# Router and token gather moved ahead of the last norm, and the experts' down weights kept in two pairs of tiles

## The reference, cut to what matters

```python
mod = silu(c) @ w_ada + b_ada                  # 6 * 1024 numbers
sh_m, sc_m, g_m, sh_f, sc_f, g_f = split(mod)
...                                            # mixer of the last block
x = x + g_m * (mixed @ w_out)
h = rms(x, norm_ffn) * (1.0 + sc_f) + sh_f     # rms: x * rsqrt(mean(x*x) + 1e-6) * norm_ffn
logits = h @ w_router + b_router               # 256 x 32
top_val, top_idx = top_k(logits, 4)
gates = softmax(top_val)
for e in range(32):                            # tokens of expert e only
    gu = h[tokens_e] @ w_gu[e] + b_gu[e]       # 1024 -> 2048
    g, u = clipped halves of gu
    act = (u + 1.0) * (g * sigmoid(1.702 * g))
    out = act @ w_dn[e] + b_dn[e]              # 1024 -> 1024
x = x + g_f * (sum over experts of gate * out)
```

## Time and profile before

| | |
|---|---|
| median of 3 runs | 1702.54 us |
| profiled execution | 1703.73 us, its span 1701.9 us |
| TensorE busy | 1580.8 us, 93% |
| VectorE, ScalarE busy | 394.1 us, 298.8 us |
| granted TensorE clock, mean | 0.98 |
| HBM read | 511.2 MB |
| expert loads | 192 pieces of 2 MB |

### The profile page before, as it was taken

One profiled execution on the slowest core, in us unless ns is written; L12 is line 12 of the kernel. 1 busy time (PEld: TensorE's weight loads), 2 busy tenths in 40 slices (PEclk: granted clock), 3 DMA queues, 4 the chain that ended last, 5 costly groups with the idle time before them and its releaser, 6 DMA issues.

```text
span 1701.9 us, 19443 instructions
## 1 busy us (share of the span) xinstructions
PE 1580.8 (93%) x7907; PEld 921.5 (54%) x7907; DVE 394.1 (23%) x889; ACT 298.8 (18%) x584; POOL 19.5 (1%) x40
## 2 busy tenths in 40 slices
PE   7989999998999999979999999989999998999995
PEld 6858787785887778853343434333333333343332
DVE  2442113412444381122111111111111111111101
ACT  1324104223222431021011101110100101011010
POOL 4000000000000000000000000000000000000000
PEclk9999999998999999979999999999999999999998
DMA  9764644546322424359999999999999999999994
GB/s 266 177 219 162 225 171 159 191 145 236 131 100 75 149 99 148 128 178 403 427 427 428 429 428 429 428 429 428 429 428 429 429 427 429 428 429 428 429 428 177
DMA packets 83752, 515.04 MB, mean 303 GB/s; under 512 B 4872, under 2 KB 8248, under 8 KB 59128
## 3 DMA queue, kind: packets, MB, share of 16 engines
q1 hardware_dynamic: 82488, 513.43, 74.9%
q0 software_dynamic: 1184, 0.92, 0.7%
q10 hardware_dynamic: 32, 0.01, 0.0%
HBM read 511.20 MB, written 3.15 MB: 302 GB/s over the span
## 4 chain that ended last, share of the span: by engine, by line
PE 73%; DMA 19%; DVE 4%; ACT 3%; issue 1%; SPq 0%; DVEq 0%; ACTq 0%
PE psum L450 25%; PE psum L1033 20%; DMA ring<-in_w_gu 16%; PE psum L1102 9%; PE psum L1006 4%; PE psum L459 3%; DMA ring<-in_w_in 2%; PE psum L1016 2%; PE psum L1024 1%; PE psum L509 1%; PE psum L490 1%; PE psum L595 1%; ACT hiddenT L1515 1%; ACT hg L1504 0%; PE psum L484 0%
## 5 line engine op out<-in xcount | busy, mean ns | idle before, releaser
L1033 PE MATMUL psum<-ring,hg 128*64 128x512 f32 x2048 | 458.7, 596 | 21.5 <-DMA ring<-in_w_gu 21.5
L450 PE MATMUL psum<-hT,ring 128*128 128x256 f32 x1504 | 337.1, 384 | 4.7 <-ACT hT L1298 4.3
L450 PEld LDWEIGHTS psum<-hT,ring 128*128 128x128 f32 x1504 | 287.5, 193 | 52.9 <-issue 13.0
L1033 PEld LDWEIGHTS psum<-ring,hg 128*64 128x64 f32 x2048 | 139.0, 137 | 312.7 <-issue 267.6
L1102 PE MATMUL psum<-w_down,hiddenT 128*64 128x512 f32 x1024 | 229.2, 600 | 28.2 <-ACT hiddenT L1515 25.2
L1102 PEld LDWEIGHTS psum<-w_down,hiddenT 128*64 128x64 f32 x1024 | 74.9, 138 | 162.1 <-issue 162.1
L1959 DVE TENSOR_SCALAR gu<-psum 128x512 f32<-128x512 f32 x32 | 22.1, 692 | 529.3 <-PE psum L1033 529.3
L1511 ACT ACTIVATE hidden<-gu 128x512 f32<-128x512 f32 x32 | 20.2, 630 | 316.4 <-DVE gu L1959 316.4
L1006 PE MATMUL psum<-pick,h_tok 128*128 128x128 f32 x512 | 63.3, 284 | 2.9 <-DVE passes L1942 2.9
L459 PE MATMUL psum<-ring,hT 128*128 128x260 f32 (+2 forms) x192 | 60.4, 470 | 6.0 <-DMA ring<-in_w_in 6.0
L1006 PEld LDWEIGHTS psum<-pick,h_tok 128*128 128x128 f32 x512 | 60.3, 197 | 8.1 <-issue 5.0
(11 more groups left out here) (381 smaller groups left out, 1170.9 us busy)
## 6 DMA issues: line engine op xcount, KB each, us to landing
ring<-in_w_gu SPq DMA_DIRECT2D x128, 2048.0 KB, 22.6
w_down<-in_w_dn SPq DMA_DIRECT2D x64, 2048.0 KB, 20.8
ring<-in_w_in SPq DMA_DIRECT2D x24, 2048.0 KB, 8.8
ring<-in_w_ada SPq DMA_DIRECT2D x12, 2048.0 KB, 9.3
ring<-in_w_out SPq DMA_DIRECT2D x6, 2048.0 KB, 7.9
ring<-in_w_in SPq DMA_DIRECT2D x2, 2064.0 KB, 16.4
ring<-in_w_ssm_o SPq DMA_DIRECT2D x2, 2048.0 KB, 8.4
ring<-in_w_in SPq DMA_DIRECT2D x1, 2112.0 KB, 12.2
```

Source lines behind the costliest of these rows:

```text
L450: mm = pe.matmul(bank[0:m, c * T:(c + 1) * T], w[:, k, c0 + c * P:c0 + c * P + m], src[:, k, :], start=(i == 0), stop=(i == k_n - 1))
L1033: mm = pe.matmul(psum[half * CAP:(half + 1) * CAP, 4 + part, :], hg[:, k, side, :], w[:, c0:c0 + 512], start=False, stop=(k == KC - 1), sk ...
```

## The change

The norm of the second half of the last block is no longer applied before router and gather. Since the norm is a factor for each token (1/rms) and a factor and a shift for each feature, it is taken apart:

- The router multiplies `xT` itself by `w_scaled`, which is `w_router` times the factor of each feature. The shift's part of the logits is added to `b_router` beforehand. The factor 1/rms of each token (`row_rstd`) multiplies the logits on VectorE.
- The eight chunks' products go to four groups of 32 columns of the array (partitions 0 to 31, 32 to 63, ...), the squares likewise; four small matmuls (`token`) add the four groups up and turn them into rows of tokens.
- `h_tok` holds the rows of `xT`. `pick` holds 1/rms in place of 1, and ScalarE applies factor and shift of each feature when it reads the gathered tokens, in eight activations instead of two.
- Factor and shift by feature in the order of the gather come from `ffn_rows`, 16 matmuls on columns of `mod_rows` taken 8 apart, and 8 for the shift's logits, behind `dt` in the last block. `b_ada` is loaded by GpSimd as 12 rows and added to `mod_rows` before it is turned; `norm_ffn` is loaded twice, once as `(c p) -> p c`, once as `(p k) -> p k`.
- The four best experts are marked with a match instead of a threshold, a running sum and a comparison.
- The matmuls with `b_dn` stand ahead of the first gather, which uses banks 6 and 7.
- The down weights have four tiles, a pair for each side (one of the four is the space of `hT` and `wide`). Both pairs are loaded before the first expert; in the loop the down pieces of an expert are loaded ahead of its gate and up pieces.

The core of the diff:

```diff
+        def ffn_rows():
+            bank = take("rows")
+            for k in range(KC):
+                lhs = mod_rows[:, k:512:KC]
+                for half in range(2):
+                    mm = pe.matmul(bank[half * HEAD:half * HEAD + HEAD, 12 * k:12 * k + 12], lhs,
+                                   K["mod_sum"][:, :], start=True, stop=True)
+            full(mm, "rows")
+            bank = take("base")
+            for k in range(KC):
+                mm = pe.matmul(bank[:, 0:NE], modT[:, 24 + k:25 + k].broadcast_to([P, P]), w_router[:, k, :],
+                               start=(k == 0), stop=(k == KC - 1))
...
-        norm_sums("f.", None)
-        pe.wait_ge(ev("h_ready"), 4 * (DEPTH + 2))
-        bank = take("router")
...
+        for c in range(KC):
+            if c % 2 == 0:
+                read_out(pe, f"wo{c // 2}")
+            q = slice(32 * (c % 4), 32 * (c % 4) + 32)
+            mm = pe.matmul(psum[q, banks["router"][0], 0:T], w_scaled[:, c, :], xT[:, c, :],
+                           start=(c < 4), stop=(c >= 4), skip_group_check=True)
...
+            if c % 2:
+                pe.wait_ge(ev("sq_d"), 4 * norm_sums.n + c // 2 + 1)
+                for c1 in (c - 1, c):
+                    q = slice(32 * (c1 % 4), 32 * (c1 % 4) + 32)
+                    mm = pe.matmul(psum[q, banks["squares"][0], 0:T], ones[:, 0:32], wide[:, c1, :],
+                                   start=(c1 < 4), stop=(c1 >= 4), skip_group_check=True)
...
         # ScalarE, gathered tokens
-                act.activation(hg[:, 4 * part:4 * part + 4, 0:width, :], bank[:, :, 0:width, :], ACT.Copy)
+                for k in range(4 * part, 4 * part + 4):
+                    ins = act.activation(hg[:, k, 0:width, :], bank[:, k % 4, 0:width, :], ACT.Identity,
+                                         bias=shift_rows[:, k:k + 1], scale=scale_rows[:, k:k + 1])
...
         # GpSimd
+        pool.dma_start(b_ada[:, :], a["b_ada_2"].rearrange("o (g n) -> (o g) n", g=12)).then_inc(ev("bcast_in"), 16)
+            pool.dma_start(norm_ffn[:, :], a["norm_ffn_2"][0].rearrange("(c p) -> p c", p=P))\
+                .then_inc(ev("bcast_in"), 16)
+        pool.dma_start(norm_ffn_rows[:, :], a["norm_ffn_2"][0].rearrange("(p k) -> p k", k=KC))\
+            .then_inc(ev("bcast_in"), 16)
...
         # SyncE
+        sp.wait_ge(ev("mixed"), 4)
+        load_down(0, 0, 0)
+        load_down(0, 0, 1)
...
+        load_down(1, 1, 0)
+        read_out(sp, "ht11")
+        read_out(sp, "token")
+        load_down(1, 1, 1)
+        next_gate_up(1, 1)
+        with sp.Fori(1, PAIRS) as i:
+            next_down(2 * i - 1, 2 * i, 0)
+            next_gate_up(2 * i, 2 * i)
+            next_down(2 * i, 2 * i + 1, 1)
+            next_gate_up(2 * i + 1, 2 * i + 1)
```

243 lines of the change are left out of this document (153 added, 90 removed).

## The result

The changed kernel is slower by 0.36%. Its median is 1706.92 us (8 runs, 1705.76 to 1709.66), that of the kernel before, run beside it, 1701.33 us (8 runs, 1699.22 to 1702.94); the ratio is 1.0036, with a 95% interval of 1.0027 to 1.0044. The forecast was 1702.5 us and no difference; the time lies inside its range, the direction was wrong. The profiled execution took 1708.47 us with a span of 1706.6 us, 4.7 us more span than before.

A forecast was written before the change was run, and what follows sets the result against it. TensorE was taken to bound the part before about 760 us, expert loads the rest, initial loads one place at the start. Terms 7.4 + 3.8 + 0.3 + 0.5 - 12.1 = -0.1 us gave 1702.5 us, range 1694.5 to 1708.5.

The forecast's parts named there:

- The form of the sum: Whole kernel: end = first free slot + pieces until last gate and up piece x 4.895 us + gaps + 35.2 us.
- Start loads, +7.4: Kernel start: `norm_ffn`'s 1024 runs of 4 bytes hold the DMA as `d_skip`'s do, delaying TensorE 7.4 us.
- Rival 1: Start: `norm_ffn` costs only what `w_router` does, 0.5 us inside the slack, kernel 1695.1 us; chance 0.17.
- ffn_rows, +3.8: Behind `dt`: 24 more TensorE matmuls, 1.7 us for the shift's logits and 2.1 for the rows; bounds 2.6 to 7.
- The router's stretch, -12.1: Projection's end to first free slot: 28.1 us instead of 40.2, so 12.1 us less; bounds -8.5 and -15.
- rival 4: Router: all 16 narrow matmuls run four abreast, 1.9 us instead of 5.2, kernel 1699.2 us; chance 0.07.
- mod, +0.3: At `mod`: adding `b_ada` first puts one more VectorE instruction (0.7 us) against 0.4 us of slack, costing 0.3 us.
- The odd expert's eight activations: Expert loop: eight ScalarE activations instead of two add 1.1 us a pair, hidden by loads except first pairs, +0.5 us.
- The tail, 35.2 us: Kernel end: work behind the last gate and up piece stays the same, 35.2 us to the end of the span.

The follow-up runs named there:

- last_swapped: Changed kernel with the last expert's two down pieces loaded behind its four gate and up pieces instead of ahead: 1705.7 us, ratio 1.0032 to the kernel before.
- pad_128: Changed kernel with an unused SBUF tile of 128 bytes a partition reserved, nothing else: 1699.2 us, ratio 0.9989 to the kernel before.
- rows_apart: Changed kernel with the 16 row matmuls as a block ahead of `xbc4`, the 8 base ones between `g0` and `g1`: 1703.1 us, ratio 1.0007.
- dt_twice: Kernel before with the 16 narrow matmuls of `dt` done twice in a row: 1707.5 us, ratio 1.0036.
- before_plus: Kernel before with `d_skip` loaded as one row and the loop over extra passes inside a branch on all engines: 1689.9 us, ratio 0.9926.
- b_dn_late: Changed kernel with the eight `b_dn` matmuls moved behind expert 0's gate and up matmuls: 1704.1 us, ratio 1.0017 to the kernel before.
- code_moved: Changed kernel with 20 unneeded 16-column matmuls added while TensorE waits for the first normalised tokens, moving its code: 1703.1 us, ratio 1.0007.
- rows_mixed: Changed kernel with the 16 row and 8 base matmuls put one by one between the wide matmuls of `g0` and `g1`: 1719.1 us, ratio 1.0102.

## Why the prediction was wrong, by its own steps

- **The form of the sum** held, with two reservations. First free slot to last piece took 908.3 us, forecast 907.4 + 0.5; last_swapped showed that fewer pieces help only where TensorE has time, and pad_128 that 4.895 us a piece is no constant.
- **Start loads, +7.4**: wrong, it cost nothing that lasted. The step that failed was to take `d_skip` as the nearest row. Rival 1 was right. The Trainium skill's rule that a strided last dimension costs one descriptor per element (page "DMA: Bandwidth & Descriptors", section "Rules for kernel authors") said the same for `norm_ffn` by its count, but the same count stands against `d_skip`, whose packets took 3.6 us each. The shorter wait for `va0` also left its 8 matmuls more of the upper clock (8.8 instead of 9.9 us). With this step right alone the forecast would have been 1695.1 and further off: its error was hidden by the others.
- **ffn_rows, +3.8**: own cost right (4.0 in rows_apart), total 8.3. Missing was the clock: no row of before had so much narrow work in a row, and the bounds of 2.6 to 7 held nothing for it. This is shown by dt_twice and rows_apart, with the reservation from before_plus that 3.6 us of narrow work can already be enough. The part that failed, 8.3 - 3.8 = 4.5 us, is nearly the whole of the 4.7 us of span.
- **The router's stretch, -12.1**: measured -6.1, outside its bounds of -8.5 to -15. Router, transposes and squares took 8.0 us instead of 6.6. The narrow matmuls cost 5.1 us as forecast (5.2): five router matmuls took 0.55 us each between transposes, and in three places a router matmul and two squares ran side by side in 0.57 us, so rival 4's mechanism is there in part. The 16 transposes took 2.9 us in pairs instead of 1.8. One of the three places (start us, us, engine line operation):

```profile
727.84 0.41 PE L1013 MATMUL psum<-spare,k_all 128*32 128x256 f32 x2
727.86 0.40 PE L999 MATMUL psum<-xT,w_scaled 128*32 128x256 f32 x1
```

  The choice came at 13.7 instead of 11.6 us, and `b_dn`, which stands in TensorE's order behind the position matmuls, started at 16.7 us where the sum had 14.0. It took 7.2 instead of 5.6, the gather 5.6 instead of 3.8: from the first work behind the idle time (739.85 us) the clock was at 0.50 for 13.9 us, not 4. These two alone are 3.3 us. The kernel before had such a stretch as well, ahead of the one in the earlier trace rows: its router matmuls, narrow ones behind 5.94 us of idle time, ran at 0.50 throughout:

```profile
730.00:734.00 4.00, 4.00 (x20) 4.00 (x21) 0.00 (x0) 0.00 (x0) 1.24 (x3) 0.50 0.85 335
```

  And the order was accepted as harmless: b_dn_late shows 4.1 us for standing in the way.
- **mod, +0.3**: 0.4 by TensorE's timeline, which is 1.5 us ahead of the kernel before at 393.6 us and 1.1 us at `dt`. That it fits is luck. At the place itself 1.8 us are lost (at 412.7 us the changed kernel is 0.3 us behind; the turning matmuls L767 took 1.76 us, partly at clock 0.50, instead of 1.06), and 1.4 us come back in the projection behind it, where the kernel before ran longer at 0.50 (416 to 420 us: 0.71 against 1.00).
- **The odd expert's eight activations**: TensorE's wait behind them is 1.70 us instead of 0.78, +0.9 for the forecast's 1.1, and stays hidden.
- **The tail, 35.2 us**: taken as unchanged, 38.1 measured. I had not looked at the code that TensorE walks through; code_moved shows the cause.

Span by span: the start came out 8.9 us under the forecast, `ffn_rows` 4.5, the router's stretch 6.0 and the tail 2.9 us over it. Errors of both signs met in a forecast that was 4.4 us off; that it was no further off, and inside the range, is luck. What turned "no difference" into a loss is that the change won 6.1 us in the router's stretch and lost 8.3 us in `ffn_rows` and 2.9 us in the tail.

## What to carry to other kernels

Price the clock with the work: count how much narrow work stands in a row, keep blocks of it short and whole with wide matmuls between them, not mixed one by one as in rows_mixed, and look at the granted clock behind each block, since even 3.6 us lowered it in before_plus. Read the last idle stretch of a kernel as code, too: an unused loop costs time by its passes and by where its code lies. Before comparing two kernels that are bound by loads, see whether the large destination tiles begin at multiples of 256 bytes; an added small tile can shift them and be taken for the effect of a change.
